# A hybrid decoder block on eight cores: weight loads moved into attention, and the last MLP group and the output norm woven together

## The reference

```python
u = rmsnorm(x) @ w_in                                  # 1024 -> 5120
y_a = (b_g * conv3(c_g * v_a)) @ w_a_out               # gated causal convolution, 512 channels
a = softmax(q1 k1) - lam * softmax(q2 k2)              # 4 heads, ALiBi, causal
y_b = (rmsnorm(a @ v) * (1 - lam_init)) @ w_b_out
x = x + (sigmoid(g_a) * y_a + sigmoid(g_b) * y_b) @ w_o
x = x + square(relu(rmsnorm(x) @ w_mlp_in)) @ w_mlp_out  # 1024 -> 4096 -> 1024
out = rmsnorm(x)
```

## Time and profile before

| what | us |
|---|---|
| median of 3 runs | 1350.09 |
| the three runs | 1347.72, 1350.09, 1370.83 |
| the profiled execution | 1347.11 |
| its span, first to last instruction, slowest core (4) | 1345.1 |
| spans of the eight cores | 1335.6 to 1345.1 |
| PE busy | 1198.4 (89%) |
| ACT, DVE busy | 637.7 (47%), 595.9 (44%) |

### The profile page before, as it was taken

How to read it: one execution, slowest core, us unless ns; L and a number is a source line. 1 busy time by engine, 2 the same in 40 slices (tenths; PEclk the granted TensorE clock), 3 DMA queues, 4 the chain that set the end, 5 groups by cost and what they waited for, 6 DMA issues and landing times.

```text
span 1345.1 us, 26999 instructions; the slowest of 8 cores (1335.6 to 1345.1 us)
## 1 busy us (share of the span) xinstructions
PE 1198.4 (89%) x7558; PEld 594.9 (44%) x7688; DVE 595.9 (44%) x995; ACT 637.7 (47%) x1009; POOL 84.8 (6%) x90
## 2 busy tenths in 40 slices
PE   4699988988999999961899999989999999999994
PEld 2345454445555455530344444444444444444441
DVE  3366434452333234410244545442644636547476
ACT  4355355658778877761457565533021021120237
POOL 1000000000000000001101111000000000000005
PEclk9899988999999999985899999999999999999998
DMA  9954020000000000029957383562124042140105
GB/s 217 192 150 141 5 33 2 2 2 2 2 2 2 2 2 2 1 85 243 143 64 92 45 103 45 69 105 32 27 38 63 1 64 34 30 64 1 32 16 234
DMA packets 64146, 80.31 MB, mean 60 GB/s; under 512 B 3168, under 2 KB 48480, under 8 KB 64000
## 3 DMA queue, kind: packets, MB, share of 16 engines
q0 software_dynamic: 53152, 44.04, 24.0%
q1 hardware_dynamic: 10848, 34.55, 7.9%
HBM read 114.24 MB, written 8.39 MB: 91 GB/s over the span
## 4 chain that ended last, share of the span: by engine, by line
PE 81%; DMA 5%; issue 4%; ACT 4%; DVE 3%; POOLq 1%; SPq 1%; POOL 0%; DVEq 0%; ACTq 0%
PE ps_all L301 62%; PE ps_all L298 10%; PE ps_all L303 7%; DMA big<-xs 2%; ACT big L574 2%; PE ps_all L324 1%; ACT big L309 1%; DMA big<-w_in 1%; DMA big<-w_b 1%; DMA big<-gmix 1%; ACT big L961 1%; SPq L288 0%; POOLq L126 0%; DVE big L318 0%; PE ps_all L622 0%
## 5 line engine op out<-in xcount | busy, mean ns | idle before, releaser
L301 PE MATMUL ps_all<-big 128*128 128x512 bf16 (+2 forms) x4286 | 946.8, 370 | 63.0 <-DMA big<-w_in 30.8
L301 PEld LDWEIGHTS ps_all<-big 128*128 128x128 bf16 x4416 | 410.7, 98 | 532.7 <-issue 92.0
L574 ACT ACTIVATE big<-ps_all,big 128x512 bf16<-128x512 f32 (+3 forms) x384 | 312.8, 867 | 107.6 <-PE ps_all L298 41.0
L936 ACT ACTIVATE big<-ps_all 128x512 bf16<-128x512 f32 x128 | 76.3, 597 | 332.1 <-PE ps_all L301 332.1
L948 DVE TENSOR_TENSOR big<-ps_all,big 128x512 f32<-128x512 f32 x256 | 176.1, 691 | 38.8 <-PE ps_all L301 35.2
L298 PE MATMUL ps_all<-big 128*128 128x129 bf16 x2176 | 175.8, 223 | 0.4 <-ACT big L574 0.4
L298 PEld LDWEIGHTS ps_all<-big 128*128 128x128 bf16 x2176 | 130.2, 99 | 44.5 <-issue 44.2
L937 DVE TENSOR_TENSOR big<-big 128x512 bf16<-128x512 bf16 x128 | 54.5, 426 | 170.5 <-ACT big L936 170.5
L303 PE MATMUL ps_all<-big 64*128 64x512 bf16 (+3 forms) x640 | 115.5, 355 | 13.7 <-ACT big L574 11.4
L309 ACT ACTIVATE big<-big 128x1024 bf16<-128x1024 f32 (+1 forms) x65 | 68.6, 1055 | 88.8 <-DVE big L308 51.8
L840 DVE TENSOR_TENSOR big<-ps_all,big 128x512 f32<-128x512 f32 x32 | 22.1, 692 | 136.1 <-PE ps_all L301 98.7
(11 more groups left out here) (57 smaller groups left out, 447.8 us busy)
## 6 DMA issues: line engine op xcount, KB each, us to landing
big<-xs SPq DMA_DIRECT2D x48, 512.0 KB, 7.7
big<-w_in POOLq DMA_DIRECT2D x36, 512.0 KB, 8.8
big<-w POOLq DMA_DIRECT2D x16, 1024.0 KB, 14.5
out<-big SPq DMA_DIRECT2D x16, 512.0 KB, 3.0
big<-w_in POOLq DMA_DIRECT2D x2, 1024.0 KB, 53.1
big<-w_in POOLq DMA_DIRECT2D x1, 2048.0 KB, 53.5
big<-w_o POOLq DMA_DIRECT2D x1, 2048.0 KB, 27.4
big<-w_a POOLq DMA_DIRECT2D x1, 1024.0 KB, 10.6
```

What stands on the lines that cost most here:

```text
L301: S.op("pe", lambda e: e.matmul(out, lhsT, rhs, start=start, stop=stop), reads=reads, writes=writes)
L574: S.op("act", lambda e, a=a, b=b, bi=bi: e.activation(PT[:, :, a:b], Sps[:, buf, :, a:b], AF.Exp, bias=btab[:, bi:bi + 1], scale=0.125), r ...
L936: S.op("act", lambda e: e.activation(r, ph, AF.Relu), reads=[phk], writes=[rk])
```

## The change

It has four parts.

1. In slice 3 the side work's rate is 56 / (128 - 40) = 0.636, so that it ends near step 77.
2. The first pair of gate weights (Wg0, Wg1) is issued when slice 3 begins, and `Wb` when the side work is out; both stood behind attention. The second pair and `Wo` stay behind attention, since Wg2 and Wg3 lie on buffers that attention uses to its end.
3. The sixteen residual loads are emitted in quarters: four behind attention, and four more after the second gates step of each of the first three slices.
4. In the last MLP group the first four `mlp_in(7)` are followed by all sixteen `mlp_out(6)`; then `mlp_in(7)`, `mlp_out(7, T)` and `final_act(T)` alternate, with `final_store` one tile behind.

```diff
@@ slice 3 of attention @@
+    def after_q():
+        S.reuse(["Wg0", "Wg1"], ["Wq"])
+        load_gate_w(0, 0)
+
+    def after_conv():
+        S.reuse(["Wb", "Wo"], ["Wc_cv", "Wc_b"])
+        wload(Wb, w_b.rearrange("(c p) n -> p c n", p=128), "Wb")
...
-            rate = cnt / (n_of_i[cur_i] - 6.0)
+            rate = cnt / (n_of_i[cur_i] - (40.0 if cur_i == 3 else 6.0))
+            if cur_i == 3:
+                after_q()
...
+        if cur_i == 3 and side["gen"] is None and stage[0] == 0:
+            stage[0] = 1
+            after_conv()
@@ behind attention @@
-    load_gate_w(0, 0)
-    wload(Wb, w_b.rearrange("(c p) n -> p c n", p=128), "Wb")
     load_gate_w(0, 1)
     wload(Wo, w_o.rearrange("(c p) n -> p c n", p=128), "Wo")
-    for T in range(16):
-        S.dma("sp", lambda e, T=T: e.dma_start(out=x_mid[:, T, :], in_=xs[T * 128:(T + 1) * 128, :]), writes=["xm%d" % T])
+    def load_x_mid(i):
+        for T in range(4 * i, 4 * i + 4):
+            S.dma("sp", lambda e, T=T: e.dma_start(out=x_mid[:, T, :], in_=xs[T * 128:(T + 1) * 128, :]),
+                  writes=["xm%d" % T])
+    load_x_mid(0)
@@ end of gates_step(i, k) @@
+            if k == 1 and i < 3:
+                load_x_mid(i + 1)
             nxt = (i, k + 2) if k < 2 else (i + 1, k - 2)
@@ the last MLP group @@
     load_w1(7)
+    for fc in range(4):
+        mlp_in(7, 0, fc)
     load_w2(7)
-    for sl in range(4):
+    for T in range(16):
+        mlp_out(6, T)
+    for sl in range(1, 5):
         for fc in range(4):
-            mlp_in(7, sl, fc)
-        for T in range(4 * sl, 4 * sl + 4):
-            mlp_out(6, T)
-    for T in range(16):
-        mlp_out(7, T)
-        final_act(T)
-        if len(fin) > 2:
-            final_store()
+            if sl < 4:
+                mlp_in(7, sl, fc)
+            T = 4 * sl - 4 + fc
+            mlp_out(7, T)
+            final_act(T)
+            if len(fin) > 1:
+                final_store()
```

More of the change, by code:

```diff
@@ L701, in side_step, with load_gate_w @@
         return True
+    R2 = region(R2_OFF, 32768)
+    wg_aps = [R2.take([128, 8, 256], BF16) for _ in range(2)]
+    Wb = R2.take([128, 4, 1024], BF16)
+    Wo = R2.take([128, 8, 1024], BF16)
+    ar = region(R1_OFF, C_OFF - R1_OFF)
+    wg_aps += [ar.take([128, 8, 256], BF16) for _ in range(2)]
+    merged = [ar.take([128, 8, 512], BF16)]
+    Wg_ring = Ring(wg_aps, "Wg")
+    gate_w = {}
+    def load_gate_w(i, k):
+        ga_t, gakey = Wg_ring.next()
+        wload(ga_t, w_cols(w_in, 3072 + 256 * k, 256), gakey)
+        gb_t, gbkey = Wg_ring.next()
+        wload(gb_t, w_cols(w_in, 4096 + 256 * k, 256), gbkey)
+        gate_w[(i, k)] = (ga_t, gakey, gb_t, gbkey)
+    def after_q():
[4 more added lines that the diff above has]
+        wload(Wb, w_b.rearrange("(c p) n -> p c n", p=128), "Wb")
     emit_qk(0)
     pvq = []
+    stage = [0]
     hold_until = 0
@@ L745, in build_program @@
             credit -= 1.0
-        if n == NS - 8:
-            pass
+        if cur_i == 3 and side["gen"] is None and stage[0] == 0:
+            stage[0] = 1
+            after_conv()
     while pvq:
@@ L753, in build_program @@
             flips.append((0, q))
-    while side_step():
-        pass
+    assert stage[0] == 1
     for c_ in chains:
@@ L758, in build_program @@
             pass
[L759 to L767, removed]
     ar = region(C_OFF, WA_OFF - C_OFF)
@@ L771, in build_program @@
     xb2_ring = Ring([ar.take([128, 1024], BF16) for _ in range(2)], "xb2_")
-    Wg_ring = Ring(wg_aps, "Wg")
-    S.reuse(["Wg0", "Wg1"], ["Wq"])
     S.reuse(["Wg2", "Wg3"] + ["mT0_%d" % d for d in range(8)], PT_ring.keys)
```

## The result

| | before | changed |
|---|---|---|
| median of six runs, us | 1348.97 | 1356.41 |
| lowest and highest, us | 1347.72, 1370.83 | 1353.29, 1404.51 |
| profiled execution, us | 1347.11 | 1355.60 |
| its span, slowest core, us | 1345.1 (core 4) | 1353.6 (core 6) |

The ratio of the times is 1.0053 [1.0037, 1.0069]. The change costs about 7 us. That is inside the range and within 2% as forecast, but the forecast stood 2 us on the other side of no change.

What follows compares the result with a forecast made beforehand. TensorE holds 81% of the last-ending chain; time can come only where it leaves TensorE: bytes behind attention, ScalarE at the end. 1347.1 - 13.5 + 0 + 1.4 + 10.8 = 1345.8, plus one: 1347 us; 8-in-10 range 1326 to 1361.

Steps and rivals of the forecast that it cites:

- The gain at 601: Behind attention: gates step (0,0) starts at 601.3 instead of 627.86, given back at the two later waits.
- the bound of -8.5: Behind attention: if POOL's 17.3 us stall stands before gate pair 1, the early loads give only -8.5 us.
- Rival 3: Behind attention: quarters hold the residual rows back, 6.3 MB leave the way to pair 2, 20 us more: 1327; chance 0.05.
- TensorE's up to 0.12 idle per step is filled: Attention, slice 3, head 0: denser side work fills TensorE's idle over some 24 steps, up to -2.9 us, taken as -2.2.
- square to addition: 0.35: Woven tail: VectorE's leg from square to addition takes 0.35 us, in rounds of 4.51, or 5.51 with a Copy.
- the term +10.8: Woven tail: the span ends at 1355.9 against 1345.1, a cost of 10.8 us.
- up to 1.7 us: Last four tiles: VectorE's scaling of the tile before may take up to 1.7 us, making a tile some 3.1.
- Rival 1: Woven tail: the weave hides the norm, tail -7.5 us, time 1328; chance 0.16.
- the ring: Woven tail: ScalarE's and VectorE's in-order lists wait on each other, so twelve rounds run at 5.0 us, not 3.45.
- Rival 2: Woven tail: idle TensorE drops to a lower clock, deciding under mean 0.69; half the rounds give +11, 1358; chance 0.16.
- Rival 4: POOL's stall falls before gate pair 1, or side work stalls at every head: +5 to +7 us, 1353; chance 0.08.

Runs made afterwards that it cites:

- experiment 11: Changed kernel with the first gate pair and Wb issued behind attention again, all else kept: 1375.05 us, ratio 1.0177 to the kernel before.
- experiment 7: Changed kernel with residual quarters 1 to 3 made to wait for the merged columns of their gates step: 1354.21 us, ratio 1.0017 to the kernel before.
- experiment 9: Changed kernel with norm one tile later, memset before additions, odd tiles scaled by VectorE, old side-work rate, residual quarters held to fourth gates step: 1312.44 us.
- experiment 5: Changed kernel with the norm one tile later and its memset ahead of the tile's additions: 1335.12 us, ratio 0.9889 to the kernel before.
- experiment 6: Changed kernel with norm one tile later, memset ahead of additions, odd tiles scaled by VectorE without Copy or POOL: 1332.95 us, ratio 0.9868.
- the old tail: Changed kernel with the last MLP group and output norm in the order of before: 1338.74 us, ratio 0.9907 to the kernel before.

## Why the prediction was right or wrong

**Part 2 was right**, in size and in mechanism. Forecast -13.5, measured -13.9 in the ledger. Counted from the first residual load, pair 1 was to land at 34.0 and step (0,1) started at 31.4 (627.60 - 596.25); step (0,2) was to start 13.5 us earlier and started at 53.0 instead of 67.7 (649.20 - 596.25; the earlier trace rows), 14.7 earlier on this core. The gain at 601 was given back at the next two waits, 11.57 and 7.94 us, because bytes are what this stretch lacks. POOL's stall of 17.3 us did not come before pair 1, so the bound of -8.5 was not used. Its cause stays open; it stood before `Wb` where `Wb` was issued right behind gate pair 0 (before, and experiment 11 with 17.27).

**Part 3 was right.** SP's row is one of sixteen loads in 12.05 us, against 12.24. Rival 3 did not happen. It put 20 us on quarters that are truly held behind the second gates step; experiment 7, which holds them there, has 7.3 in the stretch and 2 to 5 in the time. Only held to the fourth gates step (experiment 9) did the rows give 17.

**Part 1 had the right sign** and was half of what it cost: +2.8, not +1.4. The L610 rows give it head by head. From one to the next are, before, 45.92, 39.80 and 44.02; changed, 50.59, 45.86 and 38.34: +4.67, +6.06 and -5.68. To the first residual load, the rest, 28.49 became 26.30: -2.19. Head 0 got 32 x (0.636 - 0.459) = 5.7 half groups more, 5.7 x 0.86 = 4.9 us of TensorE, and grew by 4.67. The step that failed is "TensorE's up to 0.12 idle per step is filled": it gave back 0.2 us, not 2.2. The idle was there as read, but it was not filled: TensorE was busy for 42.33 of head 0's 45.92 us before and for 47.23 of 50.59 after, so 3.59 us of idle became 3.36 while its work grew by 4.90. What kept it idle I did not find. Head 1, with the same number of half groups more, grew by 6.06; heads 2 and 3 fell by 7.87, not by the whole of what left them. With head 0 at 0.2 the forecast's own terms make +3.4 against the +2.8.

**Part 4: the mechanism was right, a term of it mis-sized.** A round without a Copy was put at 4.51 and measured 4.46; the last four tiles 10.8 and 10.6 (1334.10 to 1344.67); from there to the end 9.1 and 8.9. The step that failed is the leg "square to addition: 0.35" in the rounds that have a Copy. It was read from the earlier trace rows, where POOL is idle, and carried into rounds where POOL multiplies. There it measured 2.16 (1285.30 - 1283.14), since the square takes 2.18 to 2.24, while Relu to square stayed at 0.68; and the round took 7.25 in place of 5.51. Five such rounds are 1.75 x 5 = 8.75 us too little in the term +10.8, which measured +19.1. With the 1.4 that part 1 cost more than forecast that is 10.2, near the gap of 9.8 us between the forecast sum of 1345.8 and the profiled 1355.6.

The trace of before already had a sign of it. While POOL multiplied, VectorE's scaling of an even tile took longer than the 1.28 that it takes alone. Kernel before, core 4, the timelines of POOL and VectorE:

```profile
1323.19 2.37 POOL L963 TENSOR_TENSOR big<-big 128x1024 f32<-128x1024 f32 x1 [2.17 <-ACT big L961]
```

```profile
1324.35 0.69 DVE L948 TENSOR_TENSOR big<-ps_all,big 128x512 f32<-128x512 f32 x1 [0.17 <-DVE big L948]
1324.97 1.67 DVE L966 SCALAR_TENSOR_TENSOR big<-big 128x1024 f32<-128x1024 f32 x1
```

I used this as "up to 1.7 us" for the last tiles and did not ask what else on VectorE reads two operands from SBUF. The addition beside the same multiplication (L948), with one operand from PSUM, kept 0.69. The Trainium skill (SBUF — State Buffer, Who interferes with whom) has the rule: a VectorE instruction with two inputs in SBUF contends with a GpSimd instruction that reads SBUF; it calls the port pair that the two share an exclusive lock, and says that the order of issue decides who waits. The trace agrees: the square that began 0.37 us behind the multiplication ended 0.28 us after it, as if it had waited for all of it.

**Rival 1** (the weave hides the norm, 1328) failed for the reason given against it, the ring. Experiments 5 and 6 show what it needed: the norm one tile later, its memset ahead of the additions, and no POOL beside the squares. Then Squares stand 3.45 apart and the last stretch takes 60.3 us, 7.8 under the 68.1 of before where the rival had -7.5. But part of that may come from scaling all tiles on VectorE (experiment 5, with POOL, has 63.8), and in the time experiment 6 is 5 us better than the old tail.

**Rival 2** (the clock) was seen but is not the cause. The granted clock did fall, to a mean of 0.93 and 0.84 over stretches of 20 us, between the levels of 1.2 and 2.4 GHz, behind idle times of TensorE (2.44 us before 1297.84 and 5.84 before 1308.94). But a pair of rounds takes 11.71 us at clock 1.00 and 0.93 (1286.99 to 1298.70) and 11.71 again where the mean is 0.84 (1310.40 to 1322.11). Over stretches of 5 us it went down to 0.50 (1331 to 1336), but from 1275 to 1345 the mean is 0.88, over the 0.69 from which it was to decide, and the ring hid it. **Rival 4** did not happen.

**Why the sign was missed.** The sum was -13.5 + 1.4 + 10.8 = -1.3, a small rest of large terms, so one leg of 1.75 us, met five times, decided it. A chance of faster or slower can be no surer than that rest's error.

## What to carry to other kernels

Before two in-order lists are woven, write them as a ring, with every small operation in it (a memset of 0.06 us held this one closed), and look up each leg in a row where the same neighbours are busy: here GpSimd reading SBUF beside a VectorE operation with two SBUF operands. A transfer emitted later on a queue that is idle is not held back; it needs a dependency, and where that dependency ends matters too: here it brought 2 to 5 us when it held the rows to the second gates step and 15 when it held them to the fourth, in a stretch bound by bytes. A wait filled early in such a stretch is paid at the next one, so price the last wait, not the first.

## What I had not expected of the hardware

- A bf16 square of 128 x 512 on VectorE went from 0.43 to 2.18 us beside a float32 multiplication of 128 x 1024 on GpSimd (2.33 us), five times out of five, while an addition with one PSUM operand stayed at 0.69.
- Weight loads issued beside the residual rows landed late: gate pair 1 was asked for at 606.20 and used at 627.60, while with three quarters of the rows held (experiment 9) the same pair was asked for at 601.30 and used at 613.80.
